# First two units of five stages run pair by pair, their norm behind them

## The reference

```python
# first block, two layers; h is [256, 1024]
h = h + mixer(rmsnorm(h, g))                  # layer 0 short convolution, layer 1 dilated attention
h = h + squared_relu_mlp(rmsnorm(h, g))       # mlp0, mlp1: 1024 -> 4096 -> 1024
h = h + sigmoid(rmsnorm(h, g) @ w_gate) * (p @ w_proj)
h = rmsnorm(h, norm_final)
# second block, two layers
h = h + 0.5 * swiglu(rmsnorm(h, g))           # ffn0, ffn2: 1024 -> 2 * 2816 -> 1024
u = rmsnorm(h, g)
h = h + s5_mixer(u)                           # layer 0; ends in y * sigmoid(y @ w_glu)
h = h + nsa_mixer(u, kv)                      # layer 1; kv = rmsnorm(h) @ w_kv, made after layer 0
h = h + 0.5 * swiglu(rmsnorm(h, g))           # ffn1, ffn3

def rmsnorm(x, g): return x * rsqrt(mean(x * x, -1) + 1e-6) * g
```

## Time and profile before

| | before |
|---|---|
| median of 3 runs (lowest, highest) | 1850.48 us (1846.8, 1851.46) |
| profiled execution | 1843.13 us, span 1840.9 us |
| PE busy | 1791.3 us, 97% |
| DVE, ACT, POOL busy | 1205.8, 866.4, 633.6 us |
| mean granted clock of TensorE | 0.985 |
| DMA | 336.58 MB, mean 183 GB/s |

### The profile page before, as it was taken

How to read it: one execution, slowest core, us unless ns; L and a number is a source line. 1 busy time by engine, 2 the same in 40 slices (tenths; PEclk the granted TensorE clock), 3 DMA queues, 4 the chain that set the end, 5 groups by cost and what they waited for, 6 DMA issues and landing times.

```text
span 1840.9 us, 35461 instructions
## 1 busy us (share of the span) xinstructions
PE 1791.3 (97%) x15339; PEld 1741.8 (95%) x15341; DVE 1205.8 (65%) x1380; ACT 866.4 (47%) x1096; POOL 633.6 (34%) x756
## 2 busy tenths in 40 slices
PE   8999999999999999999999989999999999999999
PEld 7899999999999999999998789999999999789999
DVE  7967667666664776686665956556655566656654
ACT  5254445544444544464444244444654446665442
POOL 6977891586753888010001720001000003420000
PEclk9999999999999999999999999999999999799999
DMA  6456566454444566657556325664456552015552
GB/s 258 179 205 216 210 216 232 161 180 170 161 172 149 178 220 216 221 210 307 191 199 220 124 78 213 225 233 174 159 152 213 208 200 103 24 49 191 197 189 109
DMA packets 53799, 336.58 MB, mean 183 GB/s; under 512 B 7899, under 2 KB 11020, under 8 KB 16908
## 3 DMA queue, kind: packets, MB, share of 16 engines
q1 hardware_dynamic: 46272, 300.00, 45.5%
q10 hardware_dynamic: 3276, 19.64, 2.8%
q0 software_dynamic: 4096, 14.68, 2.2%
HBM read 318.54 MB, written 15.75 MB: 182 GB/s over the span
## 4 chain that ended last, share of the span: by engine, by line
PE 81%; DVE 8%; POOL 4%; ACT 4%; issue 2%; DMA 1%; SPq 0%; ACTq 0%; POOLq 0%; DVEq 0%
PE psum L480 24%; PE psum L482 24%; PE psum L481 24%; DVE w_lo L1966 3%; ACT w_hi L1165 2%; DVE both L1973 1%; POOL swap L1883 1%; PE psum L1072 1%; PE psum L976 1%; ACT both L1165 1%; DVE yc L2304 1%; PE psum L1089 1%; DVE h L1979 1%; PE psum L1070 1%; POOL con L1926 1%
## 5 line engine op out<-in xcount | busy, mean ns | idle before, releaser
L480 PE MATMUL psum<-both,w_hi 128*128 128x256 f32 x3584 | 1004.4, 280 | 24.2 <-DVE both L1973 13.5
L481 PE MATMUL psum<-both,w_hi 128*128 128x256 f32 x3584 | 994.3, 277 | 0.0
L482 PE MATMUL psum<-both,w_lo 128*128 128x256 f32 x3584 | 994.3, 277 | 0.0
L1966 DVE TENSOR_TENSOR w_lo<-raw,w_hi 128x2048 fp32r<-128x2048 f32 x277 | 656.3, 2370 | 275.1 <-ACT w_hi L1165 274.6
L1165 ACT ACTIVATE w_hi<-raw 128x2048 fp32r<-128x2048 f32 (+1 forms) x281 | 536.0, 1910 | 547.0 <-PE psum L482 529.8
L480 PEld LDWEIGHTS psum<-both,w_hi 128*128 128x128 f32 x3584 | 675.9, 189 | 31.5 <-issue 12.3
L481 PEld LDWEIGHTS psum<-both,w_hi 128*128 128x128 f32 x3584 | 676.0, 189 | 0.5 <-issue 0.2
L482 PEld LDWEIGHTS psum<-both,w_lo 128*128 128x128 f32 x3584 | 675.2, 188 | 0.0
L1715 POOL TENSOR_TENSOR ssum<-sq 128x512 f32<-128x512 f32 x11 | 17.7, 1612 | 705.1 <-ACT sq L1189 705.1
L480 PE MATMUL psum<-hid_hi,w_hi 128*128 128x256 f32 x640 | 177.7, 278 | 0.5 <-ACT vcmp L1165 0.5
L481 PE MATMUL psum<-hid_lo,w_hi 128*128 128x256 f32 x640 | 176.8, 276 | 0.0
(11 more groups left out here) (389 smaller groups left out, 2091.4 us busy)
## 6 DMA issues: line engine op xcount, KB each, us to landing
raw<-in_weights SPq DMA_DIRECT2D x279, 1024.0 KB, 4.8
table<-tables ACTq DMA_DIRECT2D x8, 1792.0 KB, 9.3
tables<-st POOLq DMA_DIRECT2D x16, 512.0 KB, 5.5
tables<-st POOLq DMA_DIRECT2D x8, 256.0 KB, 6.0
tables<-turns POOLq DMA_DIRECT2D x8, 256.0 KB, 4.3
w<-in_cmp_w ACTq DMA_DIRECT2D x4, 512.0 KB, 5.4
tbl<-in_cmp_w ACTq DMA_DIRECT2D x4, 512.0 KB, 5.2
tbl<-bias_v SPq DMA_DIRECT2D x128, 16.0 KB, 4.7
```

The source lines that it names most:

```text
L480: nc.tensor.matmul(out, a_hi, b_hi, start=start, stop=False, skip_group_check=True)
L481: nc.tensor.matmul(out, a_hi, b_lo, start=False, stop=False, skip_group_check=True)
L482: return nc.tensor.matmul(out, a_lo, b_hi, start=False, stop=stop, skip_group_check=True)
L1966: tt(w_lo[:, g % RING], raw[:, g % RING], w_hi[:, g % RING].bitcast(F32), ALU.subtract).then_inc(sem["lo_ready"], 1)
```

## The change

A new function `first_two` takes the place of the first two `up_unit` calls in the five stages. It runs the two units together, into two banks, in one of two orders. `BY_PAIR` (mlp1, kv): pair 0 of both units, pair 1 of both, and so on. `PAIR_LAST` (mlp0, ffn1, ffn3): pairs 0 to 2 of the first unit, pairs 0 to 2 of the second, then pair 3 of the first and of the second. In both, `norm_sum` stands behind the last pair of the first unit, and `norm_bcast` behind the last pair of the second. In ffn1 and ffn3 the third unit goes to a third bank (`THIRD`) and no longer waits for `a_scaled`. In ffn1 the bias table comes behind both units. In sc_out and glu, ACT and DVE now split the weights of unit m + 3 behind each residual pair, so that the third split stands ahead of the fourth pair.

```diff
+            BY_PAIR = [(u, p) for p in range(PAIRS) for u in range(2)]
+            PAIR_LAST = [(u, p) for u in range(2) for p in range(PAIRS - 1)] + [(0, PAIRS - 1), (1, PAIRS - 1)]
...
+            def first_two(g0, x, banks, arrive, n, order):
+
+                for u, p in order:
+                    if p == 0:
+                        pe.wait_ge(sem["lo_ready"], g0 + u + 1)
+                    if u == 0:
+                        pe.wait_ge(arrive[0], arrive[1] + arrive[2] * (p + 1))
+                    ws = slot(g0 + u)
+                    for c in (2 * p, 2 * p + 1):
+                        for m in range(2):
+                            last = exact(banks[u][:, m * SEQ:(m + 1) * SEQ], wide(ws, c, m),
+                                         (x_hi[x][:, c], x_lo[x][:, c]), c == 0 and m == 0, c == KC - 1)
+                    if p == PAIRS - 1:
+                        last.then_inc(sem["unit_done"], 1)
+                        if u == 0:
+                            norm_sum(n)
+                        else:
+                            norm_bcast(n)
...
@@ mlp (TensorE)
-                up_unit(g, 0, x, mlp_bank(0), (sem["xl_ready"], XBASE[n], 1), lambda: norm_sum(n))
-                up_unit(g + 1, 0, x, mlp_bank(1), mid=lambda: norm_bcast(n))
+                first_two(g, x, (mlp_bank(0), mlp_bank(1)), (sem["xl_ready"], XBASE[n], 1), n,
+                          PAIR_LAST if n == R_SC else BY_PAIR)
...
@@ ffn (TensorE)
-                up_unit(g, 0, x, A_BANK, (sem["xl_ready"], XBASE[r], 1),
-                        fin_last if fin else (lambda: norm_sum(n)) if normed else None)
+                if normed and not fin:
+                    first_two(g, x, (A_BANK, B_BANK), (sem["xl_ready"], XBASE[r], 1), n, PAIR_LAST)
+                else:
+                    up_unit(g, 0, x, A_BANK, (sem["xl_ready"], XBASE[r], 1), fin_last if fin else None)
                 if f == 1:
                     bias_tables()
...
-                up_unit(g + 1, 0, x, B_BANK, mid=fin_bcast if fin else (lambda: norm_bcast(n)) if normed else None)
+                if fin or not normed:
+                    up_unit(g + 1, 0, x, B_BANK, mid=fin_bcast if fin else None)
...
-                    pe.wait_ge(sem["a_scaled"], FFN_PAIRS * f + k + 1)
-                    up_unit(g + 2, k, x, A_BANK)
+                    third = normed and not fin and k == 0
+                    if not third:
+                        pe.wait_ge(sem["a_scaled"], FFN_PAIRS * f + k + 1)
+                    up_unit(g + 2, k, x, THIRD if third else A_BANK)
...
@@ kv (TensorE)
-            up_unit(g, 0, x, U[0], (sem["xl_ready"], XBASE[n], 1), lambda: norm_sum(n))
-            up_unit(g + 1, 0, x, U[1], mid=lambda: norm_bcast(n))
+            first_two(g, x, U, (sem["xl_ready"], XBASE[n], 1), n, BY_PAIR)
...
@@ residual_stage, and the same in glu (ScalarE)
                     residual(r, m)
-                    if m < 2:
-                        split(BASE[stage] + m)
-                for m in range(2, PAIRS):
                     split(BASE[stage] + m)
...
@@ residual_stage, and the same in glu (VectorE)
                     x_low(r, m)
-                    if m < 2:
+                    if m < 3:
                         split(BASE[stage] + m)
-                split(BASE[stage] + 2)
...
@@ ffn (VectorE)
-                    tt(ta[:], two(A_BANK), rs_b, ALU.mult).then_inc(sem["a_scaled"], 1)
+                    bank = THIRD if i == 1 and f in (1, 3) else A_BANK
+                    tt(ta[:], two(bank), rs_b, ALU.mult).then_inc(sem["a_scaled"], 1)
```

More of the change, by code:

```diff
@@ L1541, in _ @@
                 residual(R_GLU, m)
-                if m < 2:
-                    split(BASE["glu"] + m)
-            for m in range(2, PAIRS):
                 split(BASE["glu"] + m)
@@ L2473, in _ @@
                 x_low(R_GLU, m)
-                if m < 2:
+                if m < 3:
                     split(BASE["glu"] + m)
-            split(BASE["glu"] + 2)
             ffn(1, R_GLU, R_FFN1, late=BASE["glu"] + 3)
```

## The result

| | before | after |
|---|---|---|
| median of 20 runs (lowest, highest) | 1848.16 us (1837.86, 1858.12) | 1854.89 us (1841.74, 1868.77) |
| ratio, 95% interval | | 1.0044 [1.0026, 1.0063] |
| profiled execution, span | 1843.13, 1840.9 us | 1841.74, 1839.6 us |

The ratio is worth some 8 us (the medians lie 6.7 apart); 1846.8 with a range up to 1852 was forecast. The profiled execution is the fastest of the 20 runs after, so its span alone can't show the loss. It shows where instructions stand.

The account below looks back on a forecast made before the run. TensorE bounds the kernel, busy 1791.3 of 1840.9 us, so only its idle time can be won. Terms +1.80 - 1.94 - 3.08 + 0.54 - 0.95 = -3.63 us take the median 1850.48 to 1846.8, range 1841.5 to 1852.

Parts of the forecast that it names:

- 48 matmuls of one unit take 120.54 - 115.10 = 5.44 us: TensorE at the five stage starts: one matmul takes 0.1133 us, a pair of a unit (12) 1.36 us.
- new wait at the broadcasts: All five stage starts: sums and 12 matmuls cover 2.30 of 2.45 us, so TensorE newly waits about 0.15 us.
- mlp1, -1.94: mlp1: waits for third and fourth pair are covered, third unit starts at 613.32, not 615.26: 1.94 us less.
- 0.4 of slack: mlp1, GpSimd's fifth table: ready at 640.1, turned at 640.52; slack falls from 4.2 to 0.4 us, still hidden.
- mlp0, +1.80: mlp0: GpSimd's late line delays table 3, TensorE waits 2.8 us for it, the stage ends 1.8 us later.
- the relu wait: First units: a later wait for `relu`, costed at nothing because the third unit's 5.44 us covers it; mlp margin 0.3.
- a sign of being wrong: mlp0, L606 near 260 us: no wait at the table, or one over 5 us, would show the forecast wrong.
- rival 1: mlp0: table 3 not late, a shorter first store gives slack; mlp0 wins 0.98, total -6.4, 1844.1 us; chance 0.22.
- ffn1, -3.08: ffn1: third unit starts at 1105.1, not 1108.21, 3.08 us less; some 1.6 of the gain is clock.
- kv, +0.54: kv: the stage moves with its broadcast, from 1289.88 to 1290.42, 0.54 us later; between 0 and 1.
- rival 3: New waits in mlp0, kv and ffn1 let the clock fall; 1.6 us per stretch, one 1848.4, three 1851.6; chance 0.12.
- ffn3, -0.95: ffn3: third unit starts at 1667.60, before 1668.55, 0.95 us less; between 0 and -1.2.

Follow-up runs that it names:

- e5: Changed kernel plus six extra broadcasts, results unread, in mlp0, mlp1, ffn1, ffn2 and ffn3: median 1856.28 us, 1.0064 of the kernel before.
- e7: Changed kernel with later broadcasts in mlp0, mlp1, ffn1, ffn3, kv in the old order, three extra unread broadcasts: 1851.58 us, 1.0043 of the kernel before.

## Why the prediction was wrong, point by point

- **The step that failed** is "48 matmuls of one unit take 120.54 - 115.10 = 5.44 us", used for all work behind the five starts: it was taken as the same after the change. It is 5.44 or 5.65, and what stands ahead of a stream decides which, by rule or by chance. The new wait at the broadcasts was foreseen with its size (0.15; measured 0.18, 0.18, 1.14 and two hidden ones) and priced at itself. Its price is the draw: up to 6.5 us or nothing per long stage.
- **mlp1, -1.94.** Up to the third unit it is -1.96 (613.20 - 600.60 against the earlier trace rows). Behind it, GpSimd's table made TensorE wait 0.81, where 0.4 of slack was forecast, and the slow pace added some 5.4 us: counted from its first matmul, the stage ended 4.7 us later instead of 1.94 earlier.
- **mlp0, +1.80.** Measured +0.3, for other reasons than forecast. The third unit came 1.08 us earlier in the stage (forecast 0.98), then the relu wait, which the prediction put at nothing, took 1.00 of it, and the table was turned at 258.90 without a wait, which was named as a sign of being wrong: rival 1 in what came of it. GpSimd's norm did start later, by 1.84 us counted from the stage's first matmul (forecast 1.8; 1.24 on the clock of the span), but its line made that up. In the timeline of GpSimd after, beside the earlier trace rows, both stores are waited for a us less, and the last power takes 0.46 us, not 2.51. Before, it began 0.20 us into a weight subtraction of VectorE (from 256.46 to 258.85); after, it is through ahead of the next one, which starts at 256.13:

```profile
125.24 0.73 POOL L1748 TENSOR_TENSOR rs_tok<-var_tok,nhalf 128x2 f32<-128x2 f32 x1 [3.59 <-DVE var_tok L2019]
...
181.40 0.40 POOL L1844 COPY ab<-bb 128x256 f32<-128x256 f32 x1 [8.28 <-DMA tables<-st]
...
229.32 1.64 POOL L1844 COPY ab<-bb 128x256 f32<-128x256 f32 x1 [3.47 <-DMA tables<-st]
...
255.51 0.46 POOL L1851 TENSOR_TENSOR st<-pw 128x128 f32<-128x128 f32 x1
```

- **ffn1, -3.08.** Half of it: -1.6. The half clock of the earlier trace rows and the memset wait went as forecast, but the wait for `w_lo` was 1.23 (forecast 0.9) and the broadcast's 1.14 (forecast 0.55, which is 2.85 less the 2.30 that sums and matmuls cover).
- **kv, +0.54.** +0.73, with the two `src` waits of 1.47 and 2.15 us (forecast 1.4 and 2.6). Behind the second the clock fell to 0.50 for 3.4 us, 1.5 us more: rival 3, once. **ffn3, -0.95**: -0.86 at the third unit, -0.7 behind it.
- **Sum.** The terms without the pace and without kv's new half clock come to 0.3 - 0.7 - 1.6 + 0.7 - 0.7 = -2.0 us (ffn1's holds the half clock that went, as its forecast did), near the forecast -3.6; that is luck in part, since mlp0 came out 1.5 us better, mlp1 and ffn1 1.2 and 1.5 worse than forecast. With mlp1's pace (5.4), kv's clock (1.5) and the 6.5 won behind 1560 it makes -1.6, and the spans differ by -1.3. The median rose because of what was no term. Nor was it among the rivals: at the prices given they end at 1851.7.
- Not settled: what in TensorE keeps the two paces, and why a half-clock stretch can change them. The paces are known from one profile per kernel (two of the changed one), not from every run; e5's and e7's loss is put down to the pace by their profiles only.

## What to carry to other kernels

A stream's duration per instruction is a measurement, not a constant: compare the mean of the same row in several stretches at the same granted clock before pricing an edit by it. Where TensorE streams for hundreds of us, what stands right ahead of the stream matters more than the few tenths it takes itself; let that instruction be reached without a wait (here by a dozen matmuls more in front of it), and count what swaps the pace. A change whose gain is 2 us can't be judged by one profile when a draw of 6.5 us and some 6 us of granted clock stand beside it: the profile after was the fastest of 20 runs.

## What the runs showed of the hardware

- Two paces for the same three-matmul sequence at full granted clock, 113.3 and 117.8 ns from start to start, kept for over a thousand matmuls.
- Without a wait the pace behind an interruption goes by rule: eight column sums lead to the slow one (102 of 104), a broadcast swaps it (100 of 100), and so do a table's 16 kernel matmuls (106 of 106) and nearly always its eight transposes (98 of 103). Behind a broadcast that waited no rule is seen (from slow, 14 fast and 15 slow).
- The mean granted clock differs between executions of one kernel, 0.982 to 0.992, and 0.001 of it goes with some 1.6 us.
